# Top four by replaced values, ranks by token block, and smaller pieces at the turn into the experts

## The chip, the cores and the metric

The kernel runs on one core of one Trainium2 chip. The metric is the device time in microseconds (us) of one execution; before the change its median over 3 runs is 1225.63 us (1223.95 to 1225.75).

## The reference, cut to what matters

One decoder layer over 256 tokens of width 1024, in f32: a Mamba-2 branch and a stick-breaking attention branch, merged by gates, a cross-attention, and then a mixture of experts, which is where the change lies:

```python
logits = (hf @ w_router + b_router)            # (256, 32)
top_v, top_i = lax.top_k(logits, 4)
gate = softmax(top_v)
# every token goes through its 4 experts, each expert:
gu  = xb @ w_gu[e] + b_gu[e]                   # 1024 -> 2048
act = min(g, 7) * sigmoid(1.702 * min(g, 7)) * (clip(u, -7, 7) + 1)
y   = act @ w_down[e] + b_down[e]              # 1024 -> 1024
# and its output is the sum of the four, weighted by gate
```

All 32 experts are used, so all their weights (12 MiB of f32 for each expert) are read once from HBM.

## The kernel before, in words

**Two stages.** The front (everything up to the router) runs until about 302 us. Its last work is the second residual `h`: TensorE transposes it and multiplies it by the router's weights (`router`, L1147), while ACT normalises it block by block (`norm_block`, L1723) and copies it to PSUM as the seed of the output (L1735, semaphore `seeded`). Tokens stand in two blocks of 128 (`b` = 0, 1).

**The turn.** VectorE (DVE) takes the logits of each block (L2141), finds the eight largest (L2143) and their indices (L2144), makes a one-hot of the four indices (L2146) and sums it to a 0/1 mask over the 32 experts (L2149). When both masks are there, TensorE counts with triangular matrices how many tokens before each one go to the same expert (L1184 to L1186), and DVE turns these counts into ranks (L2156) and into `onehot`, which says which token fills which of 64 slots of the first four experts (L2163). Between the router and the masks TensorE runs four products of ones (`ones_products(WARM[2], 4)`, L896), which serve nothing but its clock. After the counts it runs the biases of expert 0 (`bias(0)`, L1178: four products, each 32 rows by 64 columns by 512, for the gate and the up half and for two column halves), then `first_gather(0)` and `first_gather(2)` (L1209), which multiply the normalised tokens by `onehot` and so gather the first four 128-wide tiles of the four experts' inputs. DVE takes them out of PSUM (`take_gathered`, L2171, semaphore `gather_out`), and `gate_up` (L1275) runs expert 0's eight tiles `k` of 128 rows. After tile 3 it does the other four gathers (`back_gather`, L1222 and L1224).

**The experts.** Expert n's gate and up products (8 tiles, 4 products each), then the down products of expert n (L1299), the combination (L1246), the transposes (L1321) and the next expert's bias. TensorE runs all of it in the written order.

**The weight stream.** SyncE issues every load of weights in one queue, in the order of a number `m`. A load is a "pair" of 2 MiB: two k tiles of gate and up weights, [128, 2, 2048] f32, or half of the down weights. There are ten homes for pairs. Pairs 0 to 3 are expert 0's gate and up weights, 4 to 7 expert 1's, 8 and 9 expert 0's down weights; all of these are issued during the front. Pair 10 has a place of its own (`once`, over `h`), and is issued when the seeds are written (`seeded`) and the router is done. From pair 11 on each takes the home of an older pair: `pair_free(m)` waits until TensorE has done both tiles of that older pair (`chunk_used`, one increment for each two tiles). So pair 11 waits for tiles 0 and 1 of expert 0, pair 12 for tiles 2 and 3, pair 13 for tiles 4 and 5, pair 14 for tiles 6 and 7, and so on. From pair 50 on, two pairs go in one load of 4 MiB (`whole`). SyncE waits in order: nothing behind a waiting load is issued.

## Time and profile before

| | us |
|---|---|
| median of 3 runs | 1225.63 |
| lowest, highest | 1223.95, 1225.75 |
| span of the profiled execution | 1222.8 |
| TensorE busy | 1161.0 (95%) |
| VectorE busy | 302.0 (25%) |
| ScalarE busy | 245.0 (20%) |
| GpSimd busy | 235.6 (19%) |
| bytes moved | 451.56 MB, 369 GB/s over the span |

The span reaches from the first to the last instruction of one execution. The results give no separate time for that execution; 2.8 us lie between its span and the median of the runs, for what is ahead of the first instruction and behind the last. The page shows the share of the DMA engines' time at "9" (90% or more) in all slices from 320 us to the last but one.

### The profile page before, as it was taken

The numbers are of one execution on the slowest core, as the hardware profiler recorded it, in microseconds if no ns is written. First come the engines' busy times: TensorE is split into PE (matmuls) and PEld (weight loads), VectorE is DVE, ScalarE is ACT, GpSimd is POOL, SyncE is SP. The second block draws the span as 40 slices with busy tenths as digits, with TensorE's granted clock in tenths as the row PEclk, the third lists the DMA queues.
The fourth block names the chain that finished last, engine by engine and source line by source line (L and its number), as shares of the span: only waits on it lengthen the run. The fifth ranks groups of instructions, "written<-read, shape, count | busy, mean of one in ns | idle before, by whom it ended". The sixth has DMA issues, their size and how long they took to land.

```text
span 1222.8 us, 15282 instructions
## 1 busy us (share of the span) xinstructions
PE 1161.0 (95%) x6802; PEld 591.8 (48%) x6802; DVE 302.0 (25%) x463; ACT 245.0 (20%) x349; POOL 235.6 (19%) x206
## 2 busy tenths in 40 slices
PE   9999999999999999999999999989999998899996
PEld 9998878998433333333333333333333333333332
DVE  5448363224311221121122112111211211121112
ACT  6486686445101000000000000000000000000001
POOL 6979769882001000000000000000000000000000
PEclk9999999999999999999999999999999999999999
DMA  9644537848899999999999999999999999999994
GB/s 318 209 138 140 171 104 275 318 154 366 369 426 427 421 429 426 437 430 428 429 429 431 435 431 430 428 433 431 430 430 432 429 431 434 429 429 410 428 427 199
DMA packets 44702, 451.56 MB, mean 369 GB/s; under 512 B 4916, under 2 KB 5272, under 8 KB 27736
## 3 DMA queue, kind: packets, MB, share of 16 engines
q1 hardware_dynamic: 44632, 450.54, 88.8%
q8 instruction: 55, 0.90, 0.3%
q14 instruction: 15, 0.12, 0.0%
HBM read 449.48 MB, written 1.05 MB: 368 GB/s over the span
## 4 chain that ended last, share of the span: by engine, by line
PE 62%; DMA 33%; DVE 2%; ACT 1%; issue 1%; POOL 1%; DVEq 0%; ACTq 0%; POOLq 0%
DMA ring<-in_w_down 20%; PE ps L1275 19%; PE ps L1299 12%; PE ps L865 10%; DMA spare_quad<-in_w_down 7%; DMA kv_quad<-in_w_down 6%; PE ps L808 6%; PE ps L1246 3%; PE ps L1321 2%; PE ps L1178 2%; PE ps L829 1%; PE ps L1312 1%; PE ps L1197 1%; PE ps L980 1%; PE ps L889 0%
## 5 line engine op out<-in xcount | busy, mean ns | idle before, releaser
L513 POOL TENSOR_TENSOR w_parts<-ring,w_parts 128x512 fp32r<-128x512 f32 x162 | 216.9, 1373 | 42.0 <-ACT w_parts L1487 33.3
L692 POOL TENSOR_SCALAR ss<-ss 128x1 f32<-128x1 f32 (+2 forms) x8 | 1.5, 191 | 868.9 <-ACT junk L1477 864.5
L1275 PE MATMUL ps<-ring,xs 128*64 128x512 f32 x688 | 151.8, 595 | 5.8 <-DMA ring<-in_w_gu 5.8
L2216 DVE TENSOR_SCALAR xbuf<-ps 128x512 f32<-128x512 f32 x32 | 22.1, 691 | 526.4 <-PE ps L1275 526.4
L1299 PE MATMUL ps<-ring,xbuf 128*64 128x512 f32 x576 | 128.1, 595 | 17.0 <-DMA ring<-in_w_down 17.0
L1275 PE MATMUL ps<-ring,nT 128*64 128x512 f32 x560 | 123.5, 595 | 3.6 <-DMA ring<-in_w_gu 3.6
L1747 ACT ACTIVATE xbuf<-xbuf 128x512 f32<-128x512 f32 x32 | 20.2, 631 | 469.0 <-DVE xbuf L2216 469.0
L865 PE MATMUL ps<-w_parts,xT_hi 128*128 128x512 f32 x352 | 110.4, 395 | 0.0
L1275 PEld LDWEIGHTS ps<-ring,xs 128*64 128x64 f32 x688 | 47.9, 137 | 101.5 <-issue 90.3
L1487 ACT ACTIVATE w_parts<-ring 128x2048 fp32r<-128x2048 f32 x41 | 78.2, 1915 | 65.3 <-PE ps L865 39.4
L1299 PEld LDWEIGHTS ps<-ring,xbuf 128*64 128x64 f32 x576 | 43.9, 137 | 90.0 <-issue 85.2
L1757 ACT ACTIVATE xbuf<-ps 128x512 f32<-128x512 f32 x31 | 18.5, 597 | 336.5 <-PE ps L1321 336.5
L1275 PEld LDWEIGHTS ps<-ring,nT 128*64 128x64 f32 x560 | 39.2, 137 | 81.0 <-issue 73.9
L865 PEld LDWEIGHTS ps<-w_parts,xT_hi 128*128 128x128 f32 x352 | 65.3, 188 | 14.4 <-issue 0.9
L865 PE MATMUL ps<-w_parts,xT_lo 128*128 128x512 f32 x176 | 68.7, 390 | 0.0
L2232 DVE COPY xbuf<-ps 128x512 f32<-128x512 f32 x32 | 22.1, 691 | 167.7 <-PE ps L1299 167.7
L1246 PE MATMUL ps<-xbuf,scr 64*128 64x512 f32 x248 | 61.6, 615 | 0.8 <-DVE xbuf L2232 0.8
L808 PE MATMUL ps<-xT_hi,w_parts 128*128 128x256 f32 x320 | 57.9, 284 | 0.0
L1299 PE MATMUL ps<-spare_quad,xbuf 128*64 128x512 f32 x224 | 49.9, 595 | 6.7 <-DMA spare_quad<-in_w_down 6.7
L1275 PE MATMUL ps<-spare_quad,nT 128*64 128x512 f32 x240 | 53.2, 595 | 1.8 <-DMA spare_quad<-in_w_gu 1.8
L1275 PE MATMUL ps<-kv_quad,nT 128*64 128x512 f32 x224 | 49.7, 594 | 1.8 <-DMA kv_quad<-in_w_gu 1.8
L808 PEld LDWEIGHTS ps<-xT_hi,w_parts 128*128 128x128 f32 x320 | 49.9, 192 | 0.0
(312 smaller groups left out, 1314.3 us busy)
## 6 DMA issues: line engine op xcount, KB each, us to landing
ring<-in_w_gu SPq DMA_DIRECT2D x24, 4096.0 KB, 41.5
ring<-in_w_gu SPq DMA_DIRECT2D x30, 2048.0 KB, 14.8
ring<-in_w_down SPq DMA_DIRECT2D x12, 4096.0 KB, 39.7
spare_quad<-in_w_gu SPq DMA_DIRECT2D x8, 4096.0 KB, 41.5
kv_quad<-in_w_gu SPq DMA_DIRECT2D x8, 4096.0 KB, 41.6
ring<-in_w_in SPq DMA_DIRECT2D x24, 1024.0 KB, 5.2
ring<-in_w_down SPq DMA_DIRECT2D x12, 2048.0 KB, 14.7
kv_quad<-in_w_gu SPq DMA_DIRECT2D x10, 2048.0 KB, 15.0
```

Of the source, the lines that this page charges most:

```text
L513: ops.tensor_tensor(w_lo[:, m % SPLIT, c], ring_slot(m)[:, c], w_hi[:, m % SPLIT, c], ALU.subtract).then_inc(lo_ready[name], 1)
L808: i = mm(ps[:, b0 + cb // 2, (cb % 2) * T:(cb % 2 + 1) * T], w[:, k, cb * P:(cb + 1) * P], a[:, 4 * c + k, :], start=(c == 0 and k == 0 an ...
L865: i = mm(ps[:, b0 + b, :], a[:, 4 * c + k, b * P:(b + 1) * P], w[:, k, :], start=(c == 0 and k == 0 and q == 0), stop=(4 * c + k == STRIPE ...
L1178: mm(ps[64 * half:64 * half + 64, 4 + q, :], sel[quadrant(i), e, :], bgu[quadrant(i), :], start=True, stop=False, skip_group_check=True)
L1246: i = mm(ps[:, 2 * b + half, :], hot[r, b, :], yb[r, :], start=False, stop=False, skip_group_check=True)
L1275: i = mm(ps[64 * half:64 * half + 64, 4 + q, :], xg[:, k, (j % GE) * SLOTS:(j % GE + 1) * SLOTS], w[:, q * FF + half * 512:q * FF + half * ...
L1299: i = mm(ps[64 * half:64 * half + 64, 6, :], turned[:, k, :], w[:, k % 4, half * 512:(half + 1) * 512], start=(k == 0), stop=(k == FF // P ...
L1321: i = mm(ps[r, 7, c * 64:(c + 1) * 64], actv[r, c * 64:(c + 1) * 64], ident[r, r], start=True, stop=True)
L1487: af(w_hi[:, m % SPLIT, :], ring_slot(m), ACT.Copy).then_inc(hi_ready, 1)
L1747: af(sg, gl, ACT.Sigmoid, scale=ALPHA).then_inc(sg_ready, 1)
L2216: V.tensor_scalar(gl, ps[:, 4, :], LIM, None, ALU.min).then_inc(gl_ready, 1)
L2232: return V.tensor_copy(yb, ps[:, 6, :])
```

## The change

- **Top four.** `lg` becomes [128, 2, 36]; GpSimd writes -3.0e38 into the last four columns at the start (in place of the iota for `iota_e`). After `max`, DVE overwrites the lower four of the eight largest by -3.0e38 (a memset) and calls `match_replace`, which copies the logits with the eight listed values replaced by -3.2e38; one comparison with that value gives the mask. The index, the cast, the one-hot of indices and its sum go.
- **Gates.** ACT takes the exponential of all 32 logits of a block; DVE multiplies by the mask, sums, inverts and multiplies (in place of four operations on the one-hot of indices).
- **Ranks by block.** The count for block 0 needs the first mask alone and goes ahead; block 1's follows. DVE makes rank and one-hot of block 0 (semaphore `hot_half`) and then of block 1 (`hot_ready`). `first_gather(0)` takes both tiles of block 0 first, then both of block 1.
- **Products of ones.** `WARM` loses its third entry; those four products are gone.
- **Biases.** `bias(0, (0, 1))` stands between the counts of block 0 and of block 1, `bias(0, (2, 3))` after `first_gather(0)`.
- **Later gather.** `first_gather(2)` moves behind tile 0 of expert 0.
- **Torn refills.** Pairs 11 and 12 are fetched as two loads of 1 MiB each; the first waits for the first of the two tiles alone (`tile_used`), the second for both.
- The semaphore `bdn_in` is merged into `moe_in`, `rt_max` into `rt_mask`.

```diff
+TORN = (ONCE + 1, ONCE + 2)
+H2_NORMED = 2
-WARM = (18, 8, 4)
+WARM = (18, 8)
@@ SyncE
+            def fetch_torn(m, e, c):
+                rows = gate_up_rows(e, c // 2)[:, 2 * (c % 2):2 * (c % 2) + 2, :]
+                sp_.wait_ge(tile_used, TORN.index(m) + 1)
+                sp_.dma_start(main_pair(m)[:, 0, :], rows[:, 0, :]).then_inc(main_full(m), 16)
+                pair_free(m)
+                sp_.dma_start(main_pair(m)[:, 1, :], rows[:, 1, :]).then_inc(main_full(m), 16)
...
-                        if not whole(m // 2):
+                        if m in TORN:
+                            fetch_torn(m, n, c)
+                        elif not whole(m // 2):
@@ TensorE
-            ones_products(WARM[2], 4)
             pe.wait_ge(consts, N_CONST + 2)
-            pe.wait_ge(rt_mask, 2)
-            mm(ps[:, 7, 0:NE], strict_b[:], mask[:, 0, :], start=True, stop=True)
-            mm(ps[:, 7, NE:2 * NE], ones_b[:], mask[:, 0, :], start=True, stop=False)
-            mm(ps[:, 7, NE:2 * NE], strict_b[:], mask[:, 1, :], start=False, stop=True).then_inc(rk_done, 1)
+            pe.wait_ge(rt_mask, 1)
+            mm(ps[:, 6, NE:2 * NE], strict_b[:], mask[:, 0, :], start=True, stop=True).then_inc(rk_done, 1)
             pe.wait_ge(moe_in, 64)
             pe.wait_ge(sel_ready, 1)
-            bias(0)
+            bias(0, (0, 1))
+            pe.wait_ge(rt_mask, 2)
+            mm(ps[:, 7, 2 * NE:3 * NE], ones_b[:], mask[:, 0, :], start=True, stop=False)
+            mm(ps[:, 7, 2 * NE:3 * NE], strict_b[:], mask[:, 1, :], start=False, stop=True).then_inc(rk_done, 1)
...
+            def first_gather(k0, tiles=range(2)):
+                bank = 6 + k0 // 2 % 2
+                for b in range(TB):
+                    if k0 == 0 and b == 0:
+                        pe.wait_ge(hot_half, 1)
+                        pe.wait_ge(normed_act, H2_NORMED)
+                    elif k0 == 0:
+                        pe.wait_ge(hot_ready, 1)
+                        pe.wait_ge(normed_act, H2_NORMED + 1)
+                    for k in tiles:
...
@@ TensorE, gate_up
                     if k % 2:
                         i.then_inc(chunk_used, 1)
+                    elif with_gathers and k // 2 < len(TORN):
+                        i.then_inc(tile_used, 1)
+                    if with_gathers and k == 0:
+                        first_gather(2)
@@ TensorE, expert 0
                     first_gather(0)
-                    first_gather(2)
+                    bias(0, (2, 3))
@@ VectorE
-                step(V.max(out=top8[:, b, :], in_=lg[:, b, :]))
-                step(V.max_index(out=idx8[:, b, :], in_max=top8[:, b, :], in_values=lg[:, b, :]))
-                step(V.tensor_copy(idxf[:, b], idx8[:, b, 0:TOPK]))
-                step(V.tensor_tensor(oh4[:, b], ..., ALU.is_equal))
-                    V.tensor_reduce(mask[:, b], oh4[:, b]..., ALU.add).then_inc(rt_mask, 1)
+                step(V.max(out=top8[:, b, :], in_=lg[:, b, 0:NE]))
+                step(V.memset(top8[:, b, TOPK:], NO_LOGIT))
+                step(V.match_replace(out=lg_left[:, b, :], in_to_replace=top8[:, b, :], in_values=lg[:, b, :],
+                                     imm_value=TAKEN))
+                V.tensor_scalar(mask[:, b], lg_left[:, b, 0:NE], TAKEN, None, ALU.is_equal).then_inc(rt_mask, 1)
...
-            next_onehot(0, hot_ready, onehot)
+            for b, half in enumerate((hot_half, hot_ready)):
+                dve.wait_ge(rk_done, b + 1)
+                step(V.scalar_tensor_tensor(out=rankx[:, b, 0:NE], ...))
+                V.tensor_tensor(onehot[:, b], iota_b, ..., ALU.is_equal).then_inc(half, 1)
```

## Rows read from the trace of the kernel before

**Rows 1.** Windows: window, us, busy time of five engines, clock, DMA share, GB/s.
```profile
320.00:620.00 300.00, 296.84 (x1738) 111.86 (x1738) 59.60 (x89) 19.34 (x36) 4.52 (x1) 1.00 1.01 428
640.00:1150.00 510.00, 467.56 (x2714) 178.51 (x2712) 86.25 (x126) 27.53 (x55) 0.00 (x0) 1.00 1.00 429
```

**Rows 2.** Windows, same columns, 313 to 319 us.
```profile
313.00:316.00 3.00, 3.00 (x18) 1.01 (x14) 2.52 (x12) 0.00 (x0) 0.00 (x0) 1.00 0.18 76
316.00:319.00 3.00, 3.00 (x17) 0.77 (x11) 0.48 (x1) 0.00 (x0) 0.00 (x0) 1.00 0.83 262
```

**Rows 3.** Timeline of SyncE: start, us to the last issue's end, load, count.
```profile
306.63 0.33 SPq L533 DMA_DIRECT2D once<-in_w_gu  x1
315.63 3.76 SPq L533 DMA_DIRECT2D kv_quad<-in_w_gu  x2
324.75 0.33 SPq L533 DMA_DIRECT2D ring<-in_w_gu  x1
```

**Rows 4.** L533 in four windows: the issue of pairs 10 to 13, time to landing.
```profile
L533 SPq DMA_DIRECT2D once<-in_w_gu x1: 328/328/328, 306.6 to 306.6; - x1
...
DMA to landing us min/median/max: 9.8/9.8/9.8
...
L533 SPq DMA_DIRECT2D kv_quad<-in_w_gu x1: 327/327/327, 315.6 to 315.6; - x1
...
DMA to landing us min/median/max: 7.1/7.1/7.1
...
L533 SPq DMA_DIRECT2D kv_quad<-in_w_gu x1: 328/328/328, 319.1 to 319.1; - x1
...
DMA to landing us min/median/max: 8.6/8.6/8.6
...
L533 SPq DMA_DIRECT2D ring<-in_w_gu x1: 327/327/327, 324.8 to 324.8; - x1
...
DMA to landing us min/median/max: 7.8/7.8/7.8
```

**Rows 5.** The chain that ended last, 284 to 345 us: start, us, what.
```profile
305.94 1.91 PE ps L1178 x8
307.85 4.15 PE ps L1209 x16
312.00 7.02 PE ps L1275 x32
...
329.53 1.09 PE ps L1178 x8
```

**Rows 6.** Windows, columns as in rows 1, the stretch at the lower clock.
```profile
305.50:308.80 3.30, 3.10 (x14) 1.31 (x14) 1.11 (x5) 3.28 (x9) 1.15 (x1) 0.50 0.93 372
```

**Rows 7.** Timeline of VectorE: start, us, line, operation.
```profile
303.83 0.25 DVE L2141 SCALAR_TENSOR_TENSOR lg<-ps,ss,brt 128x32 f32<-128x32 f32 x1
...
304.35 0.09 DVE L2144 MATCH_VALUE_LOAD idx<-top,lg 128x8 f32 x1
304.42 0.19 DVE L2144 FIND_INDEX8 idx<-top,lg 128x8 uint32<-128x32 f32 x1
...
305.18 0.38 DVE L2149 TENSOR_REDUCE mask<-scr 128x32 bf16<-128x128 f32 x1
...
306.06 0.22 DVE L2156 SCALAR_TENSOR_TENSOR junk<-ps,mask 128x64 f32<-128x64 f32 x1 [0.43 <-PE ps L1186]
306.31 0.76 DVE L2163 TENSOR_TENSOR scr<-iota_s,junk 128x256 f32<-128x256 f32 x2
...
310.31 0.69 DVE L2171 TENSOR_TENSOR xs<-ps,gmoe 128x512 f32<-128x512 f32 x1 [3.24 <-PE ps L1209]
```

**Rows 8.** Timeline of TensorE, same columns, from the router to the counts.
```profile
300.96 2.76 PE L1147 MATMUL ps<-wr,nT 128*128 128x32 f32 x24
303.56 1.14 PE L896 MATMUL ps<-ones 128*128 128x128 f32 x8
305.70 0.18 PE L1184 MATMUL ps<-mask,strict_b 128*128 128x32 bf16 x1 [1.00 <-DVE mask L2149]
```

More of the change, by code:

```diff
@@ L222, in pair_filled @@
         return 16
-    return 16 * sum(i != ONCE and pair_sem(i) == pair_sem(m) and not (whole(i // 2) and i % 2)
-                    for i in range(m + 1 if not whole(m // 2) else m - m % 2 + 1))
+    return 16 * sum((i != ONCE and pair_sem(i) == pair_sem(m) and not (whole(i // 2) and i % 2)) + (
+        i in TORN and pair_sem(i) == pair_sem(m)) for i in range(m + 1 if not whole(m // 2) else m - m % 2 + 1))
 def last_user(m):
@@ L710, in _ @@
                            allow_small_or_imprecise_dtypes=True).then_inc(consts, 1)
-            nc.gpsimd.iota(iota_e[:], pattern=[[1, NE]], base=0, channel_multiplier=0,
-                           allow_small_or_imprecise_dtypes=True).then_inc(consts, 1)
+            nc.gpsimd.memset(lg[:, :, NE:], NO_LOGIT).then_inc(consts, 1)
             root("x", 0, 2, D, 1)
@@ L1172, in _, with bias @@
             router(1, 1).then_inc(rt_done, 1)
-            def bias(e):
-                for i in range(4):
+            def bias(e, halves=range(4)):
+                for i in halves:
                     q, half = i // 2, i % 2
@@ L1199, in gather @@
                 i.then_inc(gathered, 1)
-            def first_gather(k0):
-                if k0 == 0:
-                    pe.wait_ge(hot_ready, 1)
-                    pe.wait_ge(normed_act, 3)
-                bank = 7 - k0 // 2 % 2
-                for k in range(2):
-                    for b in range(TB):
+            def first_gather(k0, tiles=range(2)):
[8 more added lines that the diff above has]
+                    for k in tiles:
                         i = mm(ps[:, bank, k * T:(k + 1) * T], hn2[:, b, (k0 + k) * P:(k0 + k + 1) * P],
-                               onehot[:, b, :, :].rearrange("p e s -> p (e s)"), start=(b == 0), stop=(b == 1))
-                i.then_inc(gathered, 1)
+                               onehot[:, b, :, :].rearrange("p e s -> p (e s)"),
+                               start=(b == 0 and k == tiles[0]), stop=(b == 1), skip_group_check=True)
+                if 1 in tiles:
+                    i.then_inc(gathered, 1)
             def back_gather(k0):
@@ L1739, in _ @@
             af(first_hot[:], onehot.rearrange("p b e s -> p b (e s)"), ACT.Copy).then_inc(rounded, 1)
-            act.wait_ge(rt_max, 1)
+            act.wait_ge(rt_mask, 3)
             for b in range(TB):
-                af(g4[:, b, :], top8[:, b, 0:TOPK], ACT.Exp, bias=rsm[:, b:b + 1],
-                   accum_out=rsm[:, 2 + b:3 + b]).then_inc(rt_exp, 1)
+                af(lg_left[:, b, 0:NE], lg[:, b, 0:NE], ACT.Exp, bias=rsm[:, b:b + 1]).then_inc(rt_exp, 1)
             def gate(n):
@@ L2140, in _ @@
                 dve.wait_ge(rt_done, b + 1)
[L2141 removed]
+                step(V.scalar_tensor_tensor(out=lg[:, b, 0:NE], in0=ps[:, 6 + b, 0:NE],
                                             scalar=ss[:, 10 + b:11 + b], in1=brt[:], op0=ALU.mult, op1=ALU.add))
[L2143 to L2151 removed]
+                step(V.max(out=top8[:, b, :], in_=lg[:, b, 0:NE]))
[3 more added lines that the diff above has]
+                V.tensor_scalar(mask[:, b], lg_left[:, b, 0:NE], TAKEN, None, ALU.is_equal).then_inc(rt_mask, 1)
             dve.wait_ge(rt_mask, 2)
[L2154 to L2157 removed]
             iota_b = iota_s[:].unsqueeze(1).broadcast_to([P, GE, SLOTS])
@@ L2172, in take_gathered @@
                                 ALU.mult).then_inc(gather_out, 1)
-            next_onehot(0, hot_ready, onehot)
+            for b, half in enumerate((hot_half, hot_ready)):
+                dve.wait_ge(rk_done, b + 1)
+                step(V.scalar_tensor_tensor(out=rankx[:, b, 0:NE], in0=ps[:, 6 + b, (1 + b) * NE:(2 + b) * NE],
+                                            scalar=1.0, in1=mask[:, b], op0=ALU.add, op1=ALU.mult))
+                V.tensor_tensor(onehot[:, b], iota_b, rankx[:, b, 0:GE].unsqueeze(2).broadcast_to([P, GE, SLOTS]),
+                                ALU.is_equal).then_inc(half, 1)
+            V.tensor_scalar(rsm[:, 0:TB], top8[:, :, 0], -1.0, None, ALU.mult).then_inc(rt_mask, 1)
             def first_taken(k0):
                 dve.wait_ge(gathered, k0 // 2 + 1)
-                take_gathered(xgT[0], k0, 7 - k0 // 2 % 2)
+                take_gathered(xgT[0], k0, 6 + k0 // 2 % 2)
             first_taken(0)
@@ L2192, in _ @@
                 if p_:
[L2193 removed]
+                    step(V.tensor_scalar(rankx[:, :, c], rankx[:, :, 0:NE], -float(SLOTS * p_), None, ALU.add))
                 step(V.tensor_copy(gatex[:, :, c], gate_d[:]))
```

50 lines of the change are left out of this document (18 added, 32 removed).

## The prediction

> **What bounds the kernel now.** Read the windows first. From 640 to 1150 us TensorE has idle time and the DMA engines have none: share 1.00, 429 GB/s [rows 1]. From 320 to 620 us TensorE is nearly always busy, and yet the DMA engines are full there too, at 428 GB/s [rows 1]. So from 320 us to the last load the kernel runs at the rate of its weight stream, and its end stands still unless that stream gets ahead. Work of TensorE or VectorE counts only as far as it decides when a home comes free and a load can be issued.
>
> The second look is for holes in the stream. There is one just before 320 us: 76 GB/s from 313 to 316 and 262 GB/s from 316 to 319 [rows 2]. Against 429 that is short by (353 + 167) x 3 = 1560, or 1560 / 429 = 3.6 us of the stream. No edit here can give more than these 3.6 us, by any way through the stream.
>
> Third, who ends the hole. SyncE issues pair 10 at 306.63, pair 11 at 315.63, pair 12 at 319.06 (the end of the row, less one issue of 0.33) and pair 13 at 324.75 [rows 3]. Pair 11 waits for tiles 0 and 1 of expert 0, so for TensorE. The chain there is counts, bias, first gathers, gate and up [rows 5], and ahead of the counts two blocks of routing on DVE [rows 7].
>
> A rule for landings follows from rows 4. Pair 10 lands at 316.4, pair 11 at 322.8, 12 at 327.7, 13 at 332.6. Pair 12 was issued while 11 ran and lands 4.9 us behind it: 2 MiB at 429 GB/s. Pair 11 was issued at the end of the stream and lands 7.15 us after its issue, which is 4.9 plus 2.26. So a pair lands at the later of (issue + 7.15) and (former landing + 4.9). Pair 11 had (315.63 + 7.15 = 322.8) against (316.4 + 4.9 = 321.3): it costs 1.5 us. Pair 13 had (324.75 + 7.15 = 331.9) against 332.6: 0.7 us to spare. That last figure is what this forecast turns on.
>
> **The change part by part.**
>
> *Top four.* Logits, max and the step to the next operation stand: block 1's begin at 303.83 and the operation behind max at 304.35 [rows 7]. Gone per block are the index, cast, one-hot and reduce, 304.35 to 305.56. New are a memset of 4 columns (not in the trace as such; between 0 and the 0.19 of a small operation, taken as the 0.09 of the value load, its smallest row), the value load with the replace (taken as load with FIND_INDEX8, 0.26; bounds 0.1 and 0.6, since it writes 36 columns instead of 8), and a comparison (0.22 as the rank's operation; bounds 0.1 and 0.38, the reduce). With two gaps of 0.03: 304.35 + 0.12 + 0.29 + 0.22 = 304.98, against 305.56. Block 0 gains as much, but block 1's logits can't start earlier: the router ends at 303.72 [rows 8] and they start at 303.83 now. So 0.6 us, not 1.2.
>
> *Counts and ranks by block.* Block 0's count needs the first mask (about 303.2) and the end of the router, so it stands before 304. DVE then goes on at 305.02: rank 0.22, one-hot of one block 0.4 (half of the 0.76 row, plus its end), gap 0.03, so `hot_half` at 305.67 and TensorE starts at 305.81 (the 0.14 from the mask's end at 305.56 to TensorE's start at 305.70 [rows 7, 8]). Block 1's one-hot is there at 306.35, while TensorE is in block 0. Before, the gathers started at 307.85 [rows 5]. That is 2.0 us earlier, of which the bias that no longer stands there is the largest part: it was 1.91 us.
>
> *Biases.* The four products run side by side: 8 records of the bias take 1.09 us in all, and a record of 512 columns at full rate takes at least 7.02 / 32 x 2 = 0.44 us [rows 5]. Two of four should therefore take as long as four: 1.09 each time (lower bound 0.55, if time went by count). So splitting doubles the bias, from 1.09 to 2.18. The first half lies in the time in which TensorE had the products of ones and then 1.0 us of nothing [rows 8]: free. The second stands behind the first gather, where TensorE must wait for DVE to take it out, 0.69 plus about 0.2 [rows 7]: of 1.09 about 0.2 is on the path.
>
> *Clock.* From 305.5 to 308.8 the granted clock is 0.50, 1.2 GHz [rows 6], and it doubled the bias (1.91 for 1.09 [rows 5]). Ahead of its fall lay 2.76 us of router products with 32 columns, the ones, and 1.0 us idle [rows 8]. The change puts two bias products where the ones were: as much work or somewhat more, then idle again. I take the same fall and the same return at 308.8. The first gather is 8 passes of 256 columns, 0.22 us each at full rate (half of 0.44) and 0.44 at half. From 305.81 to 308.8 there is time for 6.8; the rest takes 0.3: end 309.1. With the second bias half, gate and up start at 310.2 instead of 312.0: 1.8 us earlier. Bounds: 308.5 if the clock doesn't fall, 311.9 if another such stretch follows.
>
> The Trainium skill ("TensorE: Matmul & The Clock Gate", Part 1) says that the monitor behind the clock runs freely and does not start anew with a kernel, so the point of a switch differs from run to run. One trace can't show that; by it, some executions before and after would have the fall and others not, which by the sums here is 0.7 to 1.5 us either way.
>
> *The later gather.* 8 passes, 1.76 us, are moved from ahead of tile 0 to behind it. Tile 0 ends at 310.2 + 1.76 = 311.96. Everything from tile 1 on stands 1.8 - 1.76 = 0.04 us earlier than before. The take-out of that gather (0.69) lies beside tile 1; the gate operations of DVE move behind it and end near 318, ahead of the back gathers' take-out at 320. Nobody waits for them.
>
> *Torn refills.* SyncE's order is kept. First half of pair 11: tile 0's end plus the 0.12 from a tile's end to an issue, 312.1. Second half: 315.6, as before. Halves of pair 12: 317.3 and 319.0. Pair 13: 324.7. Landings by the rule, 2.45 for 1 MiB: first half 316.4 + 2.45 = 318.9, second 321.3 (its issue gives 315.6 + 4.7 = 320.3, earlier), so pair 11 is 1.5 us earlier. Pair 12: 326.2, also 1.5 earlier. Pair 13: issue + 7.15 = 331.85, against 326.2 + 4.9 = 331.1. It lands at 331.85, which is 0.7 us earlier than 332.6. The rest of the gain is given back there, in a new small hole ahead of pair 13, because TensorE reaches tile 5 no sooner.
>
> *The rest.* The exponential over 32 columns, the merged semaphores and the memset in place of the iota lie beside other work: nothing. `once` waits for the seeds on ACT, which the change doesn't touch.
>
> **Sum.** 0.7 us off the profiled execution, whose span of 1222.8 lies 2.8 under the median 1225.63; that offset stays. 1225.6 - 0.7 = 1224.9.
>
> **Rivals.**
> 1. *The clock doesn't fall, or falls elsewhere.* Then the first gather takes 1.76 instead of 3.3 and pair 13 is issued at 323.2. It could land at 330.35; pair 12's landing allows 331.1. Gain 1.5 to 2.2: 1223.8. For: a denser pair of bias products. Against: the same idle time.
> 2. *The whole hole closes.* The loads are spread over many engines, and the last engine sets a landing; pair 13's spare time might be larger than 0.7. Then 3.6 us: 1222.0. For: pair 10 landed 9.8 us after its issue, more than 7.15, so single engines ran late [rows 4]. Against: pair 13's issue is still nearly where it was.
> 3. *Nothing moves.* If the second half of pair 11 sets the pace after all, or pair 13's spare time is 0: 1225.6.
> 4. *Slower: the lower clock lasts.* If with the ones gone the clock stays at 1.2 GHz for a second stretch of 3.3 us, TensorE loses 1.65 more, pair 13 is issued at 326.35 and lands at 333.5: 0.9 later than before, 1226.5. It decides from 0.7 us of lateness on. For: nothing but clock work was there. Against: from 305.8 on TensorE is as dense as before, and the clock came back then.
> 5. *Each torn half pays its own start.* Two more loads at 2.26 each, less 0.7: 1229.4. Against: pair 12 followed 11 by 4.9 with no such surcharge [rows 4].
>
> On the fifth the Trainium skill ("DMA: Bandwidth & Descriptors", Anatomy of one DMA) puts a fixed cost of about 2.0 us on each DMA, mostly the wait for the written bytes' receipt. Paid in series it would be an estimate of 4 us more; pair 12 shows it hidden when loads queue.
>
> **How the numbers follow.** Forecast 0.5 (own range 1224.0 to 1225.6), first rival 0.17, second 0.11, third 0.1, fourth 0.09, fifth 0.03. Range 1222.6 to 1226.6: it takes in the first, third and fourth, and comes near the second. A measurement of this kernel can't tell less than 0.2%, 2.45 us, from no change. Faster by more: the second rival and the upper part of the first, with something for what I priced too low, 0.18. Slower by more: the fifth and a worse fourth, 0.06. Within: 0.76.
>
> **What would show it.** Right: the first half of pair 11 issued near 312, pair 13 near 324.7, no window of 76 GB/s but a short dip near 325; gate and up starting near 310.2; bias in two groups of about 1.1 to 1.9 us each. Wrong: pair 13 issued before 324 or landing before 331; half clock beyond 309; a replace above 0.6 us; a gate and up start after 311.5; or a landing of a torn half more than 2.5 us behind the former.

## The result, and the profile after

| | before | after |
|---|---|---|
| median of 20 runs, us | 1224.78 | 1226.83 |
| lowest, highest | 1222.74, 1226.48 | 1225.16, 1229.06 |
| ratio after / before, 95% interval | | 1.0017 [1.0011, 1.0023] |
| span of the profiled execution | 1222.8 | 1224.2 |
| TensorE busy | 1161.0 | 1164.3 |

The changed kernel is 0.17% slower, about 2.1 us. Forecast were 0.7 us less than before, at 1224.9. The range, 1222.6 to 1226.6, ends 0.2 us below the 1226.83, and the forecast had the sign wrong. Over 20 runs the kernel before has a median of 1224.78, 0.85 lower than over the 3 runs that the forecast started from, so that the loss is larger than the distance to the range. It is smaller than the 0.2% that the prediction named as the least that can be told from no change; with 20 runs of each the interval is clear of 1 all the same.

**The turn went as forecast, in the profiled execution.** The chain that ended last, from the replace of block 1 to tile 3 (start, us, what; before, [rows 5] and [rows 7]):

```profile
304.44 0.27 DVE scr L2162 x2
...
304.74 0.19 DVE mask L2164
...
305.18 0.44 DVE scr L2187
...
305.66 3.35 PE ps L1221 x8
309.01 1.00 PE ps L1187 x4
310.02 1.87 PE ps L1289 x8
311.89 1.93 PE ps L1221 x8
313.81 5.30 PE ps L1289 x24
```

The mask is there at 304.93 (forecast 304.98), the gather starts at 305.66 (305.81), gate and up at 310.02 (310.2). Two bias products take 1.00 us (1.07 in the timeline), about as long as four do at the full clock, 1.09 [rows 5].

**The issues too.** Timeline of SyncE after (start, us, load); it answers to [rows 3]. Forecast were 312.1, 315.6, 317.3, 319.0 and 324.7 from the second line on:

```profile
306.61 0.33 SPq L533 DMA_DIRECT2D once<-in_w_gu  x1
311.93 0.33 SPq L633 DMA_DIRECT2D kv_quad<-in_w_gu  x1
315.72 0.33 SPq L635 DMA_DIRECT2D kv_quad<-in_w_gu  x1
317.44 0.33 SPq L633 DMA_DIRECT2D kv_quad<-in_w_gu  x1
319.15 0.33 SPq L635 DMA_DIRECT2D kv_quad<-in_w_gu  x1
324.83 0.33 SPq L533 DMA_DIRECT2D ring<-in_w_gu  x1
```

**The landings did not follow.** The four halves and pair 13 in the changed kernel, in the order of their issues, one window each, answering to [rows 4]:

```profile
L633 SPq DMA_DIRECT2D kv_quad<-in_w_gu x1: 328/328/328, 311.9 to 311.9; - x1
DMA to landing us min/median/max: 6.8/6.8/6.8
...
DMA to landing us min/median/max: 7.3/7.3/7.3
...
DMA to landing us min/median/max: 8.1/8.1/8.1
...
L635 SPq DMA_DIRECT2D kv_quad<-in_w_gu x1: 327/327/327, 319.2 to 319.2; - x1
DMA to landing us min/median/max: 8.9/8.9/8.9
...
L533 SPq DMA_DIRECT2D ring<-in_w_gu x1: 328/328/328, 324.8 to 324.8; - x1
DMA to landing us min/median/max: 8.1/8.1/8.1
```

The first half lands at 318.7 (forecast 318.9), the second at 323.0 (321.3), the halves of pair 12 at 325.5 and 328.1 (the second forecast at 326.2), pair 13 at 332.9 (331.85; before, 332.6). So each landing behind the first half is 1.1 to 1.9 us behind the forecast, and pairs 12 and 13 are not earlier than before at all.

**Where the bytes are.** Windows of the kernel before (window, us, busy time of five engines, clock, DMA share, GB/s):

```profile
306.00:343.00 37.00, 35.61 (x198) 14.95 (x200) 12.02 (x29) 5.44 (x11) 2.35 (x1) 0.96 0.91 378
318.00:343.00 25.00, 23.61 (x148) 9.37 (x146) 6.41 (x10) 1.50 (x3) 0.00 (x0) 1.00 1.01 431
...
336.00:337.00 1.00, 1.00 (x6) 0.29 (x4) 0.00 (x0) 0.00 (x0) 0.00 (x0) 1.00 1.12 475
```

and of the changed kernel; the first two lines answer to [rows 2]:

```profile
313.00:316.00 3.00, 3.00 (x16) 1.21 (x16) 1.84 (x9) 0.00 (x0) 0.00 (x0) 1.00 0.93 330
316.00:319.00 3.00, 3.00 (x16) 0.80 (x12) 1.57 (x7) 0.00 (x0) 0.00 (x0) 1.00 0.93 306
...
306.00:343.00 37.00, 35.61 (x192) 14.98 (x193) 10.76 (x28) 5.29 (x9) 2.35 (x1) 0.97 0.96 368
318.00:343.00 25.00, 23.61 (x146) 9.29 (x144) 6.41 (x10) 1.50 (x3) 0.00 (x0) 1.00 0.98 377
...
320.00:321.00 1.00, 1.00 (x11) 1.00 (x9) 0.69 (x1) 0.00 (x0) 0.00 (x0) 1.00 0.45 82
...
326.00:327.00 1.00, 1.00 (x8) 0.34 (x6) 0.00 (x0) 0.00 (x0) 0.00 (x0) 1.00 0.73 213
336.00:337.00 1.00, 1.00 (x6) 0.29 (x4) 0.00 (x0) 0.00 (x0) 0.00 (x0) 1.00 0.89 262
```

The hole of 76 GB/s is gone: 330 GB/s from 313 to 316, 254 more. But from 318 to 343 the stream runs at 377 GB/s instead of 431. Over 306 to 343 the changed kernel moved (378 - 368) x 37 = 370 KB less, which is 0.86 us at 429 GB/s. The ground won before 318 is given back in short dips afterwards, near 320, 326 and 336, and somewhat more. That these are the places where the stream comes to newly issued loads is a reading of the order of bytes and issues, and isn't shown. In the last of them the engines are busy for 0.89 of the time and move 262 GB/s; before, the same window shows 1.12 and 475. A share above 1 says how coarse a window of 1 us is, and the longer ones carry the reading.

That deficit is still there at the end. From 1200 to 1212 us,

```profile
1200.00:1212.00 12.00, 11.21 (x71) 4.09 (x68) 0.69 (x1) 0.87 (x2) 0.00 (x0) 1.00 0.42 175
```

is the changed kernel, which still moves 175 GB/s, and the kernel before has

```profile
1200.00:1212.00 12.00, 11.21 (x54) 3.66 (x52) 0.69 (x1) 0.16 (x1) 0.00 (x0) 1.00 0.35 145
```

30 x 12 = 360 KB: the same amount as at 343. Of the 1.4 us between the two spans this explains 0.84. In the chain that ended last, the last load of down weights lands at 1194.37 us before and at 1195.78 after, 1.41 later, and the work behind it takes as long in both. So the other 0.6 lies in that landing or ahead of it as well, and was not found.

**What the profiled execution doesn't show.** It took 1225.86 us, 1.0 under the median of its kernel. The mean granted clock over a whole run is listed for each of the 20 runs of the changed kernel: on average 0.9935, and none reached 0.997. Of 134 runs of the kernel before, taken beside the experiments, the average is 0.9960, and 46 reached 0.997. The 34 of these at 0.998 or more have a median of 1223.57 us, the 23 under 0.9945 one of 1225.02.

Two things limit what this mean can say. First, it doesn't say where the lower clock was. The profile of the changed kernel has a mean of 0.994, which is usual for its runs; the one before has 0.998, which is high for its own. Both lose the same at the turn, 0.79 from 304 to 312 us. The difference lies among the experts, where the kernel before has 1.00 throughout and the changed kernel has

```profile
904.00:912.00 8.00, 7.43 (x28) 2.95 (x30) 1.26 (x2) 0.00 (x0) 0.00 (x0) 0.79 0.98 422
...
1104.00:1120.00 16.00, 13.28 (x60) 5.09 (x60) 3.75 (x5) 0.66 (x2) 0.00 (x0) 0.89 1.00 424
```

while the stream runs on (from 1104 to 1120 the kernel before moves 424 GB/s too, and over 900 to 916 it is 434 GB/s after and 432 before). Second, at a like mean clock the changed kernel is still slower. At 0.994 or less, 13 of its runs have a median of 1227.32 us, and 23 of the kernel before 1225.02; at 0.995 and 0.996, 7 and 65 runs, it is 1226.17 and 1224.64. So the mean clock of a run accounts for a small part of the 2.1 us. A stretch at the lower clock at the turn may cost more than one elsewhere, which this mean can't tell apart.

### The profile page after: what moved, and what is told of

It reads as the page before. It is cut to its first block, busy times and chain, and to the rows that moved or that the text cites. A ratio compares the mean times of both kernels' runs of the same rounds, so it can differ in the third digit from the quotient of the medians.

```text
span 1224.2 us, 15266 instructions
## 1 busy us (share of the span) xinstructions
PE 1164.3 (95%) x6794; PEld 592.3 (48%) x6794; DVE 299.6 (24%) x462; ACT 244.9 (20%) x347; POOL 235.8 (19%) x206
## 4 chain that ended last, share of the span: by engine, by line
PE 65%; DMA 30%; DVE 2%; ACT 1%; issue 1%; POOL 1%; SPq 0%; DVEq 0%; ACTq 0%; POOLq 0%
PE ps L1289 21%; PE ps L1317 13%; DMA ring<-in_w_down 13%; PE ps L874 10%; DMA spare_quad<-in_w_down 10%; DMA kv_quad<-in_w_down 7%; PE ps L817 6%; PE ps L1260 4%; PE ps L1339 2%; PE ps L1187 2%; PE ps L838 1%; PE ps L1206 1%; PE ps L1330 1%; PE ps L989 1%; PE ps L1207 1%
## 5 line engine op out<-in xcount | busy, mean ns | idle before, releaser
L1317 PE MATMUL ps<-kv_quad,xbuf 128*64 128x512 f32 x192 | 44.4, 615 | 7.3 <-DMA kv_quad<-in_w_down 7.3
```

The costliest lines, as they stand in the source:

```text
L1317: i = mm(ps[64 * half:64 * half + 64, 6, :], turned[:, k, :], w[:, k % 4, half * 512:(half + 1) * 512], start=(k == 0), stop=(k == FF // P ...
```

## The experiments

The changed kernel and the kernel before it ran 20 times each; every other kernel ran 11 or 12 times, beside 33 or 35 runs of the kernel before on the same chip. So a ratio has an interval of about 0.09% to either side, and the difference of two such ratios one of about 0.12% (an estimate from the intervals). "Pair 11" is the issue of pair 11 (of its second half, where torn) and "clock" the granted clock from 304 to 312 us, both in its one profile; "0.997" counts the runs whose mean clock, wherever it fell, reached that. In the expectations a load "joins" the stream that is running when it is issued, and its "margin" is how long the DMA engines still have work queued at that moment.

| kernel | median | ratio, 95% interval | pair 11 | clock | 0.997 |
|---|---|---|---|---|---|
| after | 1226.83 | 1.0017 [1.0011, 1.0023] | 315.72 | 0.79 | 0 of 20 |
| e1: after, pairs whole | 1225.74 | 1.0017 [1.0008, 1.0026] | 316.75 | 0.60 | 2 of 11 |
| e2: before, two pairs torn | 1224.91 | 1.0010 [1.0001, 1.0019] | 315.00 | 0.80 | 4 of 11 |
| e3: after, six torn | 1225.39 | 1.0012 [1.0003, 1.0021] | 318.81 | 0.55 | 2 of 11 |
| e4: after, gather split | 1224.19 | 1.0002 [0.9993, 1.0011] | 313.29 | 1.00 | 0 of 11 |
| f1: before, no ones | 1225.54 | 1.0011 [1.0002, 1.0020] | 317.33 | 0.59 | 0 of 11 |
| f2: after, with ones | 1225.12 | 1.0009 [1.0000, 1.0018] | 315.68 | 0.79 | 4 of 11 |
| f4: e4, six torn | 1224.08 | 0.9993 [0.9984, 1.0002] | 316.01 | 0.60 | 4 of 11 |
| f5: e4, pairs whole | 1223.94 | 0.9995 [0.9986, 1.0005] | 314.94 | 0.79 | 1 of 11 |
| g1: routing alone | 1223.41 | 0.9992 [0.9983, 1.0000] | 313.68 | 1.00 | 5 of 12 |
| g2: before, ones doubled | 1226.58 | 1.0016 [1.0007, 1.0026] | 319.73 | 0.71 | 2 of 11 |
| g3: after, dense, whole | 1226.86 | 1.0016 [1.0008, 1.0025] | 316.97 | 0.57 | 1 of 11 |
| g4: g3, six torn | 1226.02 | 1.0005 [0.9996, 1.0014] | 317.24 | 0.57 | 3 of 12 |
| h1: g1, two torn | 1224.47 | 0.9998 [0.9989, 1.0007] | 313.50 | 1.00 | 5 of 11 |
| h2: g1, six torn | 1223.23 | 0.9987 [0.9978, 0.9996] | 313.57 | 1.00 | 3 of 11 |
| h3: g1, later gather | 1224.80 | 0.9998 [0.9989, 1.0007] | 315.03 | 1.00 | 4 of 11 |
| h4: g1, biases split | 1224.23 | 1.0001 [0.9991, 1.0010] | 315.02 | 1.00 | 6 of 11 |

### Is it the tearing? (e1, e2, e3)

e1 takes it out of the changed kernel, e2 puts it alone into the kernel before, e3 tears pairs 11 to 16.

```diff
 e1, on after
-TORN = (ONCE + 1, ONCE + 2)
+TORN = ()
 e3, on after
+TORN = tuple(range(ONCE + 1, ONCE + 7))
 e2, on before: TORN, fetch_torn and tile_used as in the change, nothing else of it
```

> The changed kernel with pairs 11 and 12 fetched whole again. Theory A (late joins: a load issued less than about 2.4 us before the DMA engines finish what is queued costs about 1 us, and the stream that runs ahead pushes pairs 13 and 15 under that margin): pair 11 is issued at 315.7, as before the change, pairs 13 and 15 have their old margins of 2.4 and 2.65 us, and the time is that of the kernel before, within 0.4 us. Theory B (the halves themselves are slow, whatever the margins): also that of the kernel before. Theory C (something else in the change costs the 2 us, in the routing or the later gather): still 1.5 to 2 us above the kernel before.

> The kernel before with nothing but pairs 11 and 12 torn. The first half of pair 11 is issued at 313.9, when the engines have just run dry (313.4). Theory A: the stream gets ahead by some 0.4 MiB, pair 13 (issued at 324.75 as before) joins with about 1.3 us of margin and costs about 1 us: 0 to 1.5 us slower than before. Theory B: 1.5 to 2.5 us slower, as the changed kernel. Theory C: the same as before or up to 0.7 us faster.

> The changed kernel with pairs 11 to 16 torn instead of 11 and 12. Theory A: the first halves of pairs 13 and 15 are issued 1.76 us earlier (323.1 and 332.6), with margins of about 2.6 and 3.4 us, so the full-rate stream isn't interrupted again behind 321 us: 1.5 to 2 us faster than the changed kernel, so 0 to 1 us faster than the kernel before. Theory B: four more torn pairs, so slower by about twice the change's loss, 3 to 6 us above the kernel before. Theory C: as the changed kernel, 2 us above.

Taken out, nothing comes back: 1.0017 again. The theory that the dips of torn loads are the whole cause falls there. Put alone into the kernel before, tearing costs 0.10% [0.01, 0.19] and gains nothing. With six torn pairs the changed kernel is at 1.0012, which is neither faster than the kernel before (theory A) nor 3 to 6 us above it (theory B); in its profile the lower clock lasts longest of all, until 315 us, and pair 11 comes at 318.81. e1's profile shows something else: the first stretch at half clock is followed by another, TensorE reaches tile 1 late, and pair 11 is issued at 316.75, 1.1 us later than in the kernel before.

```profile
304.00:312.00 8.00, 8.00 (x24) 3.60 (x26) 2.95 (x12) 5.89 (x8) 2.34 (x1) 0.60 0.96 379
```

### Is it the order at the turn? (e4, f4, f5)

```diff
 e4, on after (f5: with TORN = (); f4: with pairs 11 to 16 torn)
-            bias(0, (0, 1))
+            bias(0)
...
-                    bias(0, (2, 3))
+                    first_gather(2, (0,))
...
-                        first_gather(2)
+                        first_gather(2, (1,))
```

All four biases stand in the idle time ahead of the second count, and only the second tile of the later gather stays behind tile 0.

> The changed kernel with all four bias products in TensorE's idle time ahead of the second count (four side by side should take as long as two, 1.07 us), and with one of the two tiles of the second gather in the place of the second bias pair, the other behind tile 0. Gate and up start as in the changed kernel (309.95), all from tile 1 on is about 1.0 us earlier: pair 13 issued at 323.9, 15 at 333.4. Theory A: the margins rise from 1.1 and 1.7 to about 1.9 and 2.7 us; 0.7 to 1.7 us faster than the changed kernel. Theory B and C: at most 0.3 us faster than the changed kernel, since the torn loads and the routing stay.

> The kernel with the split second gather (which ran level with the kernel before), now with pairs 11 to 16 torn. Theory A: pair 13's first half is issued at about 320.7 instead of 322.4 and pair 15's at 330.1 instead of 331.9; the 0.8 and 0.4 us lost at these joins go: 0.7 to 1.3 us faster than with two torn pairs, so 0.5 to 1 us faster than the kernel before. Theory D: no change by that, level with the kernel before, unless the clock differs.

> The kernel with the split second gather and pairs 11 and 12 fetched whole. Tile 1 ends near 313.2, so pair 11 is issued as the engines run dry. Theory A: a restart from nearly dry costs about 1.5 us, but the later joins (13 and 15) find the engines in step and cost nothing: within 0.4 us of the kernel with two torn pairs, so tearing brings nothing net. A view in which tearing gains what it advances (1.7 us) says 1 us slower than with torn pairs.

With this order the kernel is level with the one before (1.0002, 0.9995, 0.9993; none is clear of 1). Each of the three has a partner that differs from it in this order alone: with two torn pairs 1.0002 against 1.0017 (after), with whole pairs 0.9995 against 1.0017 (e1), with six torn 0.9993 against 1.0012 (e3). These 0.15, 0.22 and 0.19% are each clear of 0.12%. So the loss sits mostly in TensorE's order between the router and tile 1, with or without torn pairs, and without any products of ones. The mean clocks don't tell the partners apart: 0.9949 (e4) and 0.9947 (f5) against 0.9948 (e1). In e4's profile the clock is 1.00 at the turn, and 0.89 from 712 to 728 and from 896 to 912 us instead.

### Are the products of ones missed? (f1, f2, g2)

```diff
 f1, on before                          g2, on before
-            ones_products(WARM[2], 4)  -WARM = (18, 8, 4)
                                        +WARM = (18, 8, 8)
 f2, on after: ones_products(4, 4) in place of bias(0, (0, 1)), ones_products(2, 5)
 behind the second count, bias(0) in place of bias(0, (2, 3))
```

> The kernel before without the four products of ones between the router and the counts (their only work is to keep TensorE busy); nothing else. Theory D (the clock: without them the lower clock comes more often or stays longer over the first gathers, and TensorE reaches tiles 1 and 5 later): 0.6 to 1.6 us slower than the kernel before, and a half-clock stretch of more than 3.5 us in the profile or in the mean clocks of the runs. Theory A (late joins of the DMA engines alone): the same time within 0.3 us, since no load is issued in another order.

> The changed kernel with products of ones again: four ahead of the second count (in the place of the first bias pair) and two behind it; all four bias products stand behind the first gather, where two take as long as four. With the same clock the path is that of the changed kernel. Theory D: the lower clock goes or shortens, 1 to 2 us faster than the changed kernel, so near the kernel before. Theory A: as the changed kernel, 1.5 to 2 us above the kernel before, since the issues of pairs 11 to 15 stand where they were.

> The kernel before with eight products of ones instead of four, so that they reach to 305.5 us, where the mask of block 1 comes, and leave no idle microsecond. Theory D: the lower clock comes less often or not over the gathers: 0.4 to 1.5 us faster than the kernel before. If the ones count for nothing: the same within 0.2 us, or up to 0.2 slower, as the counts may wait for the last one.

Yes, in the kernel before. Without them it loses 0.11% [0.02, 0.20], and none of its 11 runs reaches a clock of 0.997, where 15 of the 33 runs beside them do. In its profile the clock from 304 to 312 is 0.59 against 0.79 before, and the gathers, 4.15 us in [rows 5], take 5.88. Timeline of TensorE without the ones:

```profile
305.91 1.99 PE L1178 MATMUL ps<-front_tri,scr 32*64 32x512 f32 x8
307.82 5.88 PE L1208 MATMUL ps<-scr,xn 128*128 128x256 f32 x16
```

f2, the changed kernel with ones again, is at 1.0009 against 1.0017; the two intervals overlap, and f2 also puts the four biases together, so this doesn't show what the ones are worth there. Over all kernels: with four ones behind the router 77 of 212 runs reach 0.997 (46 of 134 of the kernel before; e2, f2, g1 and h1 to h4, 31 of 78), without them 9 of 86 (after, e1, e3, e4, f1, f4, f5).

The profiles show the turn itself. Take the time at the lower clock that the kernel before has there as one stretch. From 300 to 320 us, with four ones it is one stretch (before, e2, f2) or none (g1, h1 to h4). Without them it is one (after, f5), two (e1, f1, f4), three (e3) or none (e4). With one product (g3, g4) it is two, and with eight (g2) also two. So more than one is seen in 7 of 10 profiles of kernels that don't have the four, and in none of 8 that do.

More is not better. g2 is 0.16% slower than before, and its profile shows how:

```profile
303.76 3.65 PE L896 MATMUL ps<-ones 128*128 128x128 f32 x16
307.25 0.18 PE L1184 MATMUL ps<-mask,strict_b 128*128 128x32 bf16 x1
```

The clock fell into the filling: from 304 to 307 us it is 0.50, the eight products take 3.65 us, and the counts, whose masks have been there since 305.8, wait for them until 307.25. That pushed DVE's one-hot onto a GpSimd operation, which costs more than the wait. DVE, then GpSimd:

```profile
307.85 2.94 DVE L2163 TENSOR_TENSOR scr<-iota_s,junk 128x256 f32<-128x256 f32 x2
```

```profile
307.84 2.34 POOL L747 TENSOR_TENSOR back_lo<-xn,back_hi 128x1024 fp32r<-128x1024 f32 x1 [5.09 <-ACT back_hi L1737]
```

The same two DVE operations take 0.76 us in [rows 7]. The Trainium skill ("Perfetto Trace Analysis", Optimizing Scalar/DVE Operations) says that GpSimd and DVE share a read port of SBUF; the trace agrees, with 2.94 for 0.76 us. The 2.2 us of this collision belong to the 0.16%, so that g2 doesn't price the four further products by themselves.

### Does dense work hold the clock? (g3, g4)

```diff
 g3, on after with TORN = () (g4: with pairs 11 to 16 torn)
+            ones_products(1, 4)
             pe.wait_ge(rt_mask, 1)
...
+            bias(0, (2, 3))            # behind the second count
...
-                    bias(0, (2, 3))
+                    first_gather(2, (0,))
...
-                        first_gather(2)
+                        first_gather(2, (1,))
```

> The changed kernel with whole refills, one product of ones behind the router, the first bias pair as it stands, the second right behind the second count (no idle time ahead of the first gather, which starts about 0.5 us later), and the second gather split around tile 0. Theory D: TensorE is never idle between router and gather, so the clock falls less: faster than the same kernel with all bias products ahead of the second count (1223.94 against 1224.41 of the kernel before) by 0 to 1 us; without it 0.3 to 0.5 us slower than that.

> The same with pairs 11 to 16 torn. Theory A: with six torn pairs the joins of pairs 13 and 15 come early enough; 0.3 to 1 us faster than with whole refills, and 1 to 1.5 us faster than the kernel before. If tearing has no net use: as with whole refills, within 0.3 us.

No. In g3's profile TensorE has no idle time from 304 to 312 (first column behind the window's length), and the clock is 0.57, lower than with idle time:

```profile
304.00:312.00 8.00, 8.00 (x22) 4.23 (x18) 2.52 (x11) 5.58 (x8) 2.35 (x1) 0.57 0.94 387
```

"Fill the idle time" is not the rule. With whole pairs g3 is as slow as the changed kernel, at 1.0016, where theory D had it faster than f5 (0.9995), from which it differs in one product of ones and in where two bias products stand. With six torn pairs (g4) it is at 1.0005 and not 1 to 1.5 us below the kernel before.

### The routing alone, and one part at a time on top (g1, h1 to h4)

g1 keeps the new top four, gates and ranks by block, and gives TensorE the order of before, with whole pairs:

```diff
 g1, on after
+            ones_products(4, 4)        # ahead of the counts; then both counts, bias(0)
...
-            bias(0, (0, 1))
-                    bias(0, (2, 3))
-                        first_gather(2)
...
                     first_gather(0)
+                    first_gather(2)
 h1: g1 with pairs 11 and 12 torn; h2: g1 with pairs 11 to 16 torn
 h3, on g1: first_gather(2) behind tile 0
 h4, on g1: bias(0, (0, 1)) ahead of first_gather(0), bias(0, (2, 3)) behind it
```

> The changed kernel with TensorE's order of the kernel before (four products of ones, both counts behind both masks, all four bias products together, both first gathers ahead of tile 0) and pairs 11 and 12 whole: what is left of the change is the top four by replaced values, the gates by it and the ranks in two operations. The mask of block 1 is there 0.6 us earlier, so bias, gathers, tile 1 and pair 11 as well. Theories A and D agree here: 0.3 to 0.8 us faster than the kernel before, as the engines start in step and the clock has the ones. If the routing itself were the loss: 1 to 2 us slower.

> The version with only the routing changed (top four, gates and ranks by block; TensorE's order with the four products of ones, the four biases together and both first gathers ahead of tile 0; pairs whole), and pairs 11 and 12 torn. By itself that version was 0.9992 [0.9983, 1.0000] of the kernel before. Joins theory (what tearing advances is given back, and a bit more, where pairs 13 and 15 join engines that are out of step): 0.9992 + 0.0010, from the kernel before with the same edit at 1.0010, so 1.0002, 1224.6. Rival, tearing is worth nothing either way, as the changed kernel against itself with whole pairs (1.0017 both): 0.9992, 1223.4. Rival, the prediction's own step (pair 13 lands 0.7 us earlier): 0.9986.

> As the former with pairs 11 to 16 torn: a candidate to beat both kernels. If the loss comes at the first whole pair behind torn ones, tearing six moves it back to pair 17 and nothing is gained: 0.9992 to 1.0002. If the smaller pieces keep the ground that the stream has at 320 us: up to 2 us, 0.9976. From the two cases so far in which six were torn instead of none or two (0.9993 against 0.9995; 1.0005 against 1.0016) I expect 0.9989, 1223.1.

> The version with only the routing changed, and the second first gather behind tile 0; ones and biases as before, pairs whole. Pair 11 waits for tiles 0 and 1, both gathers lie ahead of tile 1 either way, so by the order of work nothing moves: 0.9992. If the mix on TensorE matters for the clock, gate and up products come 1.8 to 3.5 us earlier and the second stretch at 1.2 GHz becomes likelier or less likely: 0.9985 to 1.0003.

> The version with only the routing changed, and the biases as two pairs: two ahead of gather 0, two behind it (ones kept, both gathers ahead of tile 0, pairs whole). At full clock the split doubles 1.09 us, so pair 11 comes 1.1 us later, and the 0.9992 becomes 1.0001, 1224.5, if pair 11's issue sets the end; at 1.2 GHz each pair takes 1.9 and it is 1.0009. Rival, the split is hidden as in the prediction: 0.9992 to 0.9994.

The routing alone is at 0.9992 [0.9983, 1.0000], faster by its median and at the edge of its interval. Its TensorE, from the ones to gate and up:

```profile
303.62 1.14 PE L905 MATMUL ps<-ones 128*128 128x128 f32 x8
305.16 0.18 PE L1193 MATMUL ps<-mask,strict_b 128*128 128x32 bf16 x1 [0.40 <-DVE mask L2162]
...
305.31 1.09 PE L1187 MATMUL ps<-front_tri,scr 32*64 32x512 f32 x8
306.33 3.72 PE L1221 MATMUL ps<-scr,xn 128*128 128x256 f32 x16
309.98 7.09 PE L1289 MATMUL ps<-kv_quad,xs 128*64 128x512 f32 x32
```

The idle time ahead of the counts is 0.40 us, against 1.00 in [rows 8], and the clock does not fall: the bias takes 1.09 and not 1.91. Pair 11 is issued at 313.68, 1.95 us earlier than before. In the profiles of all five kernels with the new routing and the four ones ahead of both counts (g1, h1 to h4) the clock is 1.00 from 304 to 312; in the two with the old routing and four ones (before, e2) it is 0.79 and 0.80. As these are single profiles, and the means over the runs of g1 (0.9966) and of before (0.9960) differ little, this is a hint and no proof.

What is clear is the distance from g1 to the changed kernel, 0.9992 to 1.0017. The 0.25%, within about 0.1% to either side, is what the rest of the change costs in one: ones out, biases split, gather later, pairs torn.

The parts on top of g1, one at a time. None of the single differences is clear of 0.12%, so they show a direction and the profile's times, and no price:
- two torn pairs (h1): 0.9998, +0.06%;
- the later gather (h3): 0.9998, +0.06%. Ahead of tile 0 TensorE now waits 0.78 us for DVE to take the first gather out, which the second gather had covered, and pair 11 is issued at 315.03, 1.35 later than in g1 (0.16 of it was there ahead of the bias). I had expected that nothing moves;
- the split biases (h4): 1.0001, +0.09%. 1.07 us twice instead of 1.09 once; pair 11 at 315.02, again 1.3 later, 0.17 of it from ahead of the bias;
- six torn pairs (h2): -0.05%. At 0.9987 [0.9978, 0.9996] it is the best kernel here and clear of 1.

The later gather in TensorE's timeline, h3:

```profile
306.48 1.99 PE L1221 MATMUL ps<-scr,xn 128*128 128x256 f32 x8
309.26 1.94 PE L1289 MATMUL ps<-kv_quad,xs 128*64 128x512 f32 x8 [0.78 <-DVE xs L2179]
```

The tearing is read best here, because pair 11's issue is the same within 0.2 us in g1, h1 and h2. Windows of g1 (pairs whole), h1 (two torn), h2 (six torn):

```profile
313.00:318.00 5.00, 5.00 (x28) 2.15 (x25) 0.91 (x4) 0.00 (x0) 0.00 (x0) 1.00 0.72 259
318.00:343.00 25.00, 23.61 (x144) 8.86 (x145) 6.42 (x10) 1.50 (x3) 0.00 (x0) 1.00 1.01 431
```

```profile
313.00:318.00 5.00, 5.00 (x30) 2.19 (x26) 0.78 (x3) 0.00 (x0) 0.00 (x0) 1.00 0.97 313
318.00:343.00 25.00, 23.61 (x145) 8.76 (x145) 6.41 (x10) 1.50 (x3) 0.00 (x0) 1.00 1.00 409
```

```profile
313.00:318.00 5.00, 5.00 (x29) 2.19 (x26) 0.84 (x3) 0.00 (x0) 0.00 (x0) 1.00 0.95 318
318.00:343.00 25.00, 23.61 (x143) 8.76 (x144) 6.41 (x10) 1.50 (x3) 0.00 (x0) 1.00 1.01 424
```

Two torn pairs win (313 - 259) x 5 = 270 KB, 0.63 us, up to 318, and lose (431 - 409) x 25 = 550 KB, 1.28 us, afterwards: net 0.65 us lost, and the medians say 0.06%, 0.7 us. Six win 0.69 and lose 0.41: net 0.3 gained, where the medians say 0.05%, 0.6 us, within the intervals.

The same edits were made on four orders of TensorE's work. Two torn pairs against whole ones: 0.00 (after, e1), +0.10 (e2), +0.07 (e4, f5), +0.06% (h1, g1). Six against whole ones: -0.05 (e3, e1), -0.02 (f4, f5), -0.11 (g4, g3), -0.05% (h2, g1). The means, +0.06 and -0.06%, each have about 0.06% to either side, an estimate: the signs agree, and each size is about as large as its noise.

## Why the prediction was wrong

**What held.** Where the kernel is bound, and by whom the hole is ended. In the nine kernels with whole pairs, the earlier pair 11 is issued in the one profile, the lower the ratio, with little out of order: 313.68 (0.9992), 314.94 (0.9995), 315.02 (1.0001), 315.03 (0.9998), 315.63 (before, 1), 316.75 (1.0017), 316.97 (1.0016), 317.33 (1.0011), 319.73 (1.0016). The cost of the replace (0.27 for load and replace, forecast 0.29), the mask's 0.6 us, the bias that takes as long for two products as for four, and each time of the turn were right to 0.2 us for the profiled execution.

**The step that failed in the profiled execution: the rule for landings.** "Later of issue + 7.15 and former landing + 4.9" came from whole pairs in a stream that had just restarted, and was used for halves. It gave 331.85 for pair 13 and with it the whole gain of 0.7 us. Everything ahead of it came as forecast, the issue at 324.83 and the clock included, and pair 13 landed at 332.9, 0.3 later than before. Landings came 1.1 to 1.9 us later than by the rule, 0.86 us less had been moved by 343, and the span grew by 1.4 us. The fifth rival had the right sign and the wrong size and place: it is no start for each half (the first lands as forecast) but a few dips further on. Torn loads ahead aren't needed for such a miss. With whole pairs the rule gives pair 13's landing within 0.2 us in before, e1, g1, h3 and h4, but in f5 it gives 332.2, and pair 13, issued at 324.06, took 9.6 us and landed at 333.7. There the stream lost less: 425 GB/s from 318 to 343.

How much of the 0.17% is the tearing is less clear. On the kernel before it costs 0.10% by itself (e2), on g1 0.06% by the medians (h1). On the changed kernel, taking it out changed nothing (e1, both 1.0017). The intervals are 0.06 and 0.09% to either side, so a cost of 0.06% isn't contradicted there, and it isn't shown.

**The step that a single profile couldn't carry: "I take the same fall and the same return at 308.8."** In the profiled execution it happened nearly so, half clock from 305.0 to 308.4:

```profile
305.00:308.40 3.40, 2.94 (x9) 2.30 (x10) 1.18 (x5) 3.40 (x6) 0.76 (x1) 0.50 0.93 366
```

How the clock went at the turn in the other 19 runs of the changed kernel no row shows. Of the profiles of its seven relatives without four ones, five have two or three stretches (e1, e3, f4, g3, g4), f5 has one and e4 none; f1, the kernel before without them, has two. The fourth rival, the lower clock that lasts, named this mechanism; I gave it 0.09. Its 1226.5 lies near the measured 1226.83 by luck: it was 0.9 above the 1225.6 that it started from, and measured are 2.1 above 1224.78. Against it I held that TensorE is dense from 305.8 on. g3 shows that density there doesn't decide. f1 shows that in the kernel before the ones do: 0.11% for removing 1.14 us of work that computes nothing. I had priced that edit at nothing, because two bias products stood in the same place; f1 has nothing in that place, so what the exchange costs in the changed kernel is likely of that kind and isn't shown. By its own terms the step's bounds for gate and up were 308.7 and 311.5, and not 308.5 and 311.9 (first gather and bias pair at full clock, 1.76 + 1.09, or at half, twice that, from 305.81). The Trainium skill ("TensorE: Matmul & The Clock Gate", Part 1) says that the monitor runs freely, so that switches fall differently from run to run; the runs agree, with means of 0.990 to 0.999 for the kernel before, and this is why one profile could not carry the step.

**The third: "everything from tile 1 on stands 0.04 us earlier."** Compared with the order of before this is nearly right: pair 11's second half was issued at 315.72, where pair 11 had 315.63. What it hid is that in g1's profile, with the clock at 1.00, the routing by itself puts pair 11 nearly 2 us earlier, and that the later gather and the split biases each give some 1.2 us of this back (h3, h4). At the same clock of 0.79, f5 issues pair 11 at 314.94, 0.8 earlier than the changed kernel. I set the parts against the kernel before, and not each against the rest of the change.

**The sum.** Routing -0.08, ones gone +0.11, biases split +0.09, later gather +0.06, two torn pairs +0.06 to +0.10: together +0.24 to +0.28%, against +0.17 measured. Each has 0.09 to 0.12% to either side, and in the changed kernel the later gather and the split overlap (the second bias pair stands in the 0.78 us in which h3 waits for DVE), so the agreement is no better than rough.

**What stays open.** Why the lower clock lasts for none, one, two or three stretches at the turn. No row tells what makes the difference; only how often it is seen with and without the ones is shown, in one profile of each kernel. Nor is it shown how much of the 0.17% is clock and how much is order. That it is one of the two, and not the tearing alone, e1 and the three pairs of kernels beside e4, f4 and f5 show.

## What to carry to other kernels

A product that computes nothing may be what keeps a clock: here four of them were worth 0.11% in the kernel before. Before it is removed, price it by taking it out alone, over many runs, and not by one profile. When a change has parts, set each against the others and not against the old kernel: here one part gained 0.08% by its median, and the others together gave 0.25% back. And where a stream is advanced by cutting loads smaller, look at how much it moves behind them and not only at the first issues: cutting two lost 0.06%, cutting six of the same stream gained 0.06%, as means over four orders, each about as large as its noise.

## What the hardware showed that I had not expected

- Behind torn loads the stream can dip while the engines count as busy: share 0.89 at 262 GB/s from 336 to 337 in the changed kernel, and over 318 to 343 a share of 1.00 at 409 GB/s in h1. With whole pairs it is 431 GB/s there, before and in g1, but 425 in f5. That the 16 engines are out of step behind torn loads, and that this is the cause, is my reading and wasn't tested by itself. A rival is untested too: a stream that runs ahead has less queued when pair 13 is issued.
- The lower clock isn't tied to the turn: the changed kernel has it again at 904 to 912 and 1104 to 1120 us, the kernel before doesn't, and the mean clock of a run adds them all up.
- TensorE busy for 8.00 of 8.00 us had a clock of 0.57 (g3) and 0.60 (e1); busy for 7.60, it had 1.00 (g1).
- Two DVE operations beside one of GpSimd: 2.94 us instead of 0.76.
